# In the second token group x is loaded whole, x1 and h stay on chip, and the residual, norm and gelu work is placed anew

## The reference

```
mod = silu(cond) @ w_ada + b_ada -> sh1, sc1, g1, sh2, sc2, g2
h   = rms_norm(x, norm1_g) * (1 + sc1) + sh1
z   = h @ w_in            # q, k, v of two attentions, and gate logits
merged = sigmoid(ga) * (o_g @ w_branch_a) + sigmoid(gb) * (o_d @ w_branch_b)
x1  = x + g1 * (merged @ w_out)
h2  = rms_norm(x1, norm2_g) * (1 + sc2) + sh2
q   = h2 @ peer_w_query   # 8 heads, two halves of 128
per token and head: scores against 2 x 128 sub keys, the 16 best pairs -> expert ids, softmax weights
a   = gelu(h2 . peer_u[id]);  peer = sum (a * weight) * peer_v[id]
y   = rms_norm(x1 + g2 * peer, final_norm_g)
```

## Time and profile before

| | before |
|---|---|
| median of 3 runs | 5130.7 us (5129.67 to 5141.64) |
| the profiled execution | 5127.9 us, of which the span of the trace is 5126.2 us |
| PE, DVE, POOL, ACT busy | 65%, 53%, 36%, 9% |
| mean granted TensorE clock | 0.773 of full speed |
| bytes moved | 1885.14 MB, mean 368 GB/s |
| u and v gathers (software queue) | 1347.98 MB |
| weights and other transfers of SP | 535.33 MB |

### The profile page before, as it was taken

One profiled execution on the slowest core, in us unless ns is written; L12 is line 12 of the kernel. 1 busy time (PEld: TensorE's weight loads), 2 busy tenths in 40 slices (PEclk: granted clock), 3 DMA queues, 4 the chain that ended last, 5 costly groups with the idle time before them and its releaser, 6 DMA issues.

```text
span 5126.2 us, 33046 instructions
## 1 busy us (share of the span) xinstructions
PE 3345.8 (65%) x11402; PEld 1296.8 (25%) x11402; DVE 2718.6 (53%) x4111; ACT 455.3 (9%) x824; POOL 1835.9 (36%) x1365
## 2 busy tenths in 40 slices
PE   5969988999787798899988293333333333333334
PEld 0333343444344443444443141000000000000000
DVE  2320139986133202566758768565656556565653
ACT  0010010000222101111110011000000000000000
POOL 0000014432232000243534445545545564545542
PEclk7979999999899999999998696555555555555555
DMA  9979987997998688888989998999999999999997
GB/s 376 381 272 353 371 302 293 344 356 314 406 366 322 239 288 295 351 354 345 383 340 397 358 391 321 422 421 421 421 414 416 421 421 421 418 413 421 421 421 318
DMA packets 412276, 1885.14 MB, mean 368 GB/s; under 512 B 30544, under 2 KB 34160, under 8 KB 241760
## 3 DMA queue, kind: packets, MB, share of 16 engines
q0 software_dynamic: 187200, 1347.98, 64.6%
q1 hardware_dynamic: 224928, 535.33, 28.2%
HBM read 1845.08 MB, written 39.42 MB: 368 GB/s over the span
## 4 chain that ended last, share of the span: by engine, by line
DMA 52%; PE 27%; DVE 11%; issue 6%; POOL 3%; ACT 1%; SPq 0%; DVEq 0%; POOLq 0%; ACTq 0%; PEldq 0%
DMA activations<-in_peer_v,zt 33%; PE ps L821 20%; DMA big<-in_peer_u,sel 5%; DMA big<-in_peer_v,zone 4%; DMA big<-in_w_in 3%; DMA big<-in_peer_v,sel 2%; DVE big L1657 2%; DMA big<-in_w_ada 2%; PE ps L1167 2%; DMA big<-in_w_out 1%; DVE big L1604 1%; PE ps L921 1%; PE ps L981 1%; PE ps L872 1%; POOL big L753 1%
## 5 line engine op out<-in xcount | busy, mean ns | idle before, releaser
L821 PE MATMUL ps<-big,activations 128*128 128x512 f32 x4096 | 1809.3, 602 | 103.2 <-DMA big<-in_w_out 36.7
L1937 DVE CUSTOM_DVE_ANT_0 big<-big,activations 128x2048 f32<-128x2048 f32 x384 | 876.5, 2290 | 710.2 <-DMA big<-in_peer_u,sel 710.1
L821 PEld LDWEIGHTS ps<-big,activations 128*128 128x128 f32 x4096 | 781.7, 193 | 1114.7 <-issue 1017.3
L1167 PE MATMUL ps<-activations,zt 128*32 128x512 f32 x1536 | 354.3, 1014 | 569.9 <-DMA activations<-in_peer_v,zt 569.9
L805 POOL DMA_INDIRECT big<-in_peer_u,sel x384 | 501.1, 1305 | 603.4 <-DVE zt L1937 513.6
L1167 PE MATMUL ps<-big,zt 128*32 128x512 f32 x1536 | 328.8, 981 | 400.7 <-DMA big<-in_peer_v,zt 298.5
L1592 DVE CUSTOM_DVE_ANT_0 big<-big 128x2048 f32<-128x2048 f32 x128 | 291.5, 2292 | 128.0 <-DMA big<-in_peer_u,sel 113.4
L1604 DVE SCALAR_TENSOR_TENSOR big<-big,work 128x2048 f32<-128x2048 f32 x128 | 301.0, 2352 | 83.7 <-DMA big<-in_peer_v,sel 80.7
L809 POOL DMA_INDIRECT big<-in_peer_v,zt x192 | 279.0, 1453 | 177.9 <-PE ps L1167 128.8
L753 POOL DMA_INDIRECT big<-in_peer_u,sel x128 | 214.5, 1676 | 329.2 <-DVE work L1592 270.9
L753 POOL DMA_INDIRECT big<-in_peer_v,sel x128 | 237.9, 1859 | 254.6 <-DVE big L1604 186.7
(11 more groups left out here) (193 smaller groups left out, 2452.8 us busy)
## 6 DMA issues: line engine op xcount, KB each, us to landing
big<-in_w_in SPq DMA_DIRECT2D x84, 2048.0 KB, 10.3
big<-in_w_ada SPq DMA_DIRECT2D x48, 2048.0 KB, 12.8
big<-in_w_out SPq DMA_DIRECT2D x24, 2048.0 KB, 13.0
big<-in_peer_w_query SPq DMA_DIRECT2D x24, 2048.0 KB, 9.5
big<-in_w_branch_a SPq DMA_DIRECT2D x12, 2048.0 KB, 12.5
big<-in_w_branch_b SPq DMA_DIRECT2D x12, 2048.0 KB, 9.4
big<-z_blocks SPq DMA_DIRECT2D x20, 512.0 KB, 12.2
big<-in_peer_u,sel POOLq DMA_INDIRECT x640, 13.2
```

The lines of the kernel that those rows point to most:

```text
L821: ins = nc.tensor.matmul(bank(bk), acts[:, k, b * P:(b + 1) * P], w[:, n % WS, k], start=(start and k == 0), stop=(stop and k == KT // 2 - 1))
L1167: ins = nc.tensor.matmul(ps[32 * j:32 * j + 32, q * 512:(q + 1) * 512], spread[(t - 1) % 2][:, k * 32:(k + 1) * 32], v_slot(m)[:, j * CH:( ...
L1937: V.tensor_tensor_reduce(out=x, in0=x, in1=h_of[ph], scale=1.0, scalar=0.0, op0=ALU.mult, op1=ALU.add, accum_out=dots_s[t % 2][:, k:k + 1] ...
```

## The change

In group 2 only, and at the start and the end of the last stage:

- x of the three blocks is loaded whole (three transfers of 1 MB) as soon as the branch units are done, together with the rows of the second norm; the twelve pieces per chunk are gone. g1 comes after, and DVE waits for it at the first residual instead of before step 12.
- `residual_2` adds into the x buffer on chip, so that x1 stays there, and a third instruction takes the sum of squares of the chunk. x1 is still stored to `x1d`, for the last stage.
- `norm_2` adds up the four sums, takes the root, waits until the block's four stores of x1 have landed, and writes h over x1. The loads of x1, the stores of h and the loads of h are gone: `h_of` are the same buffers.
- The residuals stand at hand-picked places in steps 12 and 13 (`beside`), the norms at the 18th, 22nd and 24th place of step 13; step 14 has none. The gelus of ACT move with them.
- In the last stage the v buffers are free from the start (two of them are others than before); the final of block 0 moves from the end of step 0 to the fifth dot of step 1, and POOL waits for it before v gather number 6, because the gate row lies in that buffer. SP waits for it before it loads the rows and x1 pieces of the quarters.
- For the last block, PE does the sums of quarters 0 to 2 between the products of the last step.

```diff
@@ SP, group 2
+                    sp.wait_ge(mm_done, U_OUT[2])
+                    for lb in range(n):
+                        sp.dma_start(xb[lb], xs[block_of(g, lb)]).then_inc(G["xt"][lb], 16)
+                    sp.dma_start(A, mod[cnd:cnd + 1, 4 * D:5 * D].to_broadcast([P, D])).then_inc(s["row"], 16)
+                    sp.dma_start(Bv, mod[cnd:cnd + 1, 3 * D:4 * D].to_broadcast([P, D])).then_inc(s["row"], 16)
...
-                        sp.dma_start(zn(D + lb * CH, CH), xs[block_of(g, lb)][:, c * CH:(c + 1) * CH]).then_inc(G["xt"][lb], 16)
...
-                    for lb in range(2):
-                        sp.dma_start(xb[lb], x1d[block_of(g, lb)]).then_inc(s["x"][lb], 16)
-                    for lb in range(n):
-                        sp.wait_ge(s["h"], lb + 1)
-                        sp.dma_start(h2d[lb], h).then_inc(h2_out, 16)
...
-                        sp.wait_ge(t_done, 4 * (T_H[2] + GROUP[2]))
-                        sp.wait_ge(h2_out, 16 * GROUP[2])
-                        sp.dma_start(h_of[0], h2d[0]).then_inc(h_in[0], 16)
+                        sp.wait_ge(s["h"], n)
+                        sp.dma_start(fin_x, x1d[0]).then_inc(fa_in, 16)
@@ POOL, last stage
+                        if m == VR - V_LATE:
+                            pool.wait_ge(y_ready, 2)
@@ PE, last stage
+                    if t == STEPS_3 and k in (6, 10, 14):
+                        last_fold((k - 6) // 4)
@@ ACT, group 2
-                        if g == 2 and v in (2, 8):
-                            step = PH + 4 + v // 6
+                        elif v >= 4:
+                            sa.wait_ge(G["ou"], B * DCH + v - 3)
+                        if g == 2 and v in (0, 8):
+                            step = PH + 4 + v // 8
@@ DVE
+                def residual_2(v):
+                    c, lb = v // n, v % n
+                    x1 = nbuf[2][0][lb][:, c * CH:(c + 1) * CH]
+                    if v == 0:
+                        dve.wait_ge(G["g1"], 16 * (1 + B))
+                    dve.wait_ge(bank_free, U_OUT[2] + v + NB + 1)
+                    link(V.tensor_tensor(zt[:, v % 4], zt[:, v % 4], zn(c * CH, CH), ALU.mult))
+                    if c == 0:
+                        dve.wait_ge(G["xt"][lb], 16)
+                    link(V.tensor_tensor(x1, x1, zt[:, v % 4], ALU.add))
+                    signal(V.tensor_tensor_reduce(out=zt[:, v % 4], in0=x1, in1=x1, ..., accum_out=small[:, 40 + 4 * lb + c:41 + 4 * lb + c]), G["ou"], B * DCH + v + 1)
+                def norm_2(lb):
+                    link(V.tensor_reduce(small[:, 2:3], small[:, 40 + 4 * lb:44 + 4 * lb], AX.X, ALU.add))
+                    signal(V.tensor_scalar(small[:, 0:1], small[:, 2:3], 1.0 / D, EPS, ALU.mult, ALU.add), nrm_ms, nth)
+                    dve.wait_ge(nrm_rs, nth)
+                    link(V.reciprocal(small[:, 3:4], small[:, 1:2]))
+                    dve.wait_ge(G["br_st"][lb], 16 * 2 * DCH)
+                    link(V.scalar_tensor_tensor(x1[lb], x1[lb], small[:, 3:4], A, ALU.mult, ALU.mult))
+                    signal(V.tensor_tensor(x1[lb], x1[lb], Bv, ALU.add), nrm[2]["h"], lb + 1)
...
+                    beside = ({15: [(residual_2, 0)], 16: [(residual_2, 1)], 17: [(residual_2, 2)],
+                               25: [(residual_2, 3)], 27: [(residual_2, 4)], 30: [(residual_2, 5)]},
+                              {8: [(residual_2, 6)], 10: [(residual_2, 7)], 12: [(scale_row,)], 13: [(residual_2, 8)],
+                               18: [(residual_2, 9), (norm_2, 0)], 20: [(residual_2, 10)], 22: [(residual_2, 11), (norm_2, 1)],
+                               24: [(norm_2, 2)]})
...
+            dve.sem_inc(v_free, VR)
...
+                    if k == 4 and t == 1:
+                        dve.wait_ge(fa_in, 112)
+                        final(fin_x, fin_gate, fin_gain, 2)
...
-                if t == 0:
-                    dve.wait_ge(fa_in, 112)
-                    final(ac(A1, D), ac(A1 + D, D), ac(A1 + 2 * D, D), 2)
-                    dve.sem_inc(v_free, VR)
```

More of the change, by code:

```diff
@@ L91 @@
 UR, VR = 8, 8
+V_LATE = 2
 U_EARLY = WS * HALF // D
@@ L1406, in _ @@
                         scored(v - 2)
-                    if g == 2 and v == 8:
-                        top_exps(2 * PH)
-                        gelus(1, (PH + 7) * 2 * TOPK)
+                    if g == 2 and v in (2, 9):
+                        step = PH + 6 + v // 9
+                        top_exps(step + 1)
+                        gelus(1, step * 2 * TOPK)
                 if g < 2:
```

92 lines of the change are left out of this document (43 added, 49 removed).

## The result

| | before | after |
|---|---|---|
| median | 5130.85 us (5129.67 to 5141.64, 4 runs) | 5088.77 us (5080.02 to 5095.19, 4 runs) |
| profiled execution, its span | 5127.9, 5126.2 us | 5090.43, 5088.5 us |
| bytes | 1885.14 MB | 1875.70 MB |

The ratio is 0.9913, 95% interval 0.9899 to 0.9928: faster by 42 us, where 56 was forecast. Run again later (the tenth experiment), the kernel after gave 0.9919.

A forecast was written before the change was run, and what follows sets the result against it. The last stage is byte-bound; before it, DVE's stops fill the ring of four gathers and halt POOL. Steps 37, hand-over 9 and end 10 sum to 56 us: 5075 us, own range 5062 to 5086, eight in ten 5052 to 5102.

The forecast's parts named there:

- Step 12: Block 0's expert step 12: without the g1 wait, dots begin near 2609 and the step ends at 2737, against 2748.
- two queues taking turns: Step 12's dots: gathers and SP's large rows alternate, 10 transfers each in 50 us, the last dot ending at 2669.
- Step 13: Block 0's step 13 takes over the norms, with a 5.9 us store wait: 138 us, ending at 2875 against 2862.
- Steps 14 and 15: Block 0's last two steps: ends at 2988 and 3089, say 3090, 37 us earlier than 3127.
- the 2.9 with 7.5 for its loads: Step 14: 32 gathers at 2.9 us, choice 12.7, and 7.5 us for three 1 MB loads for the final.
- I take 2.75 us for a gather: Step 15, with weights nearly through: 88 us of gathers plus 12.7 of choice, 101 us.
- The rival of the unchanged rate: Gathers and weights together stay at 364 GB/s, step 15 ends at 3107, total 5092 us; chance 0.2.
- PE: Beside DVE's steps: query projection starts near 2862, scores end at 3047, 43 us ahead of step 15.
- the slower rival: More gathers starve PE's weights; at 36 us for each half the program takes 5178 us; chance 0.03.
- The hand-over: Start of the last stage: early v gathers and the moved final give 9 us beyond the steps' 37.
- The drain in front of v6: Hand-over: the DMA drains for some 17 us while POOL waits for the final; today about as long before v0.
- The end: Kernel's end: three of four last-block quarters pass between the last 16 products, saving 10 us, 4 as the low end.

The follow-up runs named there:

- the tenth experiment: The kernel after, unchanged, run again beside the kernel with later norms and the final in step 0: 5091.0 us, ratio 0.9919 to the kernel before.
- experiment 5: The kernel before with one edit, DVE waiting for g1 at its first residual instead of ahead of step 12: 5140.83 us, ratio 1.0011.
- experiment 8: The kernel after, with POOL issuing each gather of step 15 one buffer later, three in flight instead of four: 5108.35 us, ratio 0.9943.
- experiment 7: The kernel after, with SP also storing the three h blocks (3.1 MB) that nobody reads: 5091.72 us, ratio 0.9915 to the kernel before.
- experiment 2: The kernel after, with the final of block 0 behind step 0 again and the v buffers freed only there: 5097.93 us, ratio 0.9937.
- experiment 4: The kernel after, with the final of block 0 before the fifth dot of step 0 instead of step 1: 5085.41 us, ratio 0.9912.
- experiment 1: The kernel after, with all four sums of the last block behind PE's last product again: 5096.3 us, ratio 0.9926 to the kernel before.

## Why the prediction was right, and where it was off

The median of 5088.8 us lies in the wide range, 5052 to 5102, and outside the forecast's own, 5062 to 5086; it is 14 us above the forecast.

**Step 12** began at 2607.4, forecast 2609, and ended at 2740.9, forecast 2737. The forecast of two queues taking turns was right to the row: 4.97 us from dot to dot, and the last dot ended at 2670, forecast 2669. The reason for the gain was only half right. I put the gain down to the wait for g1, and experiment 5 shows that this wait covered a longer one, for PE's first unit; without the new places the edit is worth nothing. My sum used both edits, so its number stood; for the reason that I gave, that was luck.

**Step 13** ended at 2876.4, forecast 2875, and its store wait was 6.8 us, forecast 5.9. The Trainium skill's two terms for a transfer ("DMA: Bandwidth & Descriptors", anatomy of one DMA) give an estimated 2.6 us here, which would have made the wait 5 us too short. The page fitted them to transfers issued from GpSimd, which these stores, issued by SP, are not. The trace doesn't agree with them beside other transfers: the twelve stores took 9.2 us in the median.

**Steps 14 and 15** are where the forecast failed: 118.3 and 108.7 us against 113 and 102, 12 of the 13 us by which the steps fell short of 3090 (step 12 was longer, its start earlier and step 13 shorter than forecast, 1 us net). The steps that failed are "I take 2.75 us for a gather" in step 15, and in step 14 the 2.9 with 7.5 for its loads. They failed for two reasons.

In step 15 a gather took 2.9 to 3.0 us. I took the pace from the DMA's side: fewer bytes beside it, so faster gathers. The DMA is not full there (share 0.88, 339 GB/s), and experiment 8 takes one buffer away and the step grows by 18 us: the round of four buffers limits the pace. At the 421 GB/s of the last stage the step's 36.9 MB would take 88 us, by estimate, and with the 12.7 of the choice 100, about my number; the ring took the rest.

In step 14 the DMA is full, and by the one profile of experiment 7 the bytes do set the length. My 113 us for them ask for more than any rate seen here: the 48.0 MB of the step in 113 us are 425 GB/s. The error lies in the 2.9, from which I had taken off six residuals, 8.7 us, as if they had been on the path. They stood in a step whose DMA was full already (share 1.01 in the earlier trace rows), so taking them away could save little. Without that subtraction the step would be 114 + 7.5 = 121.5 us, by estimate; it was 118.3.

The rival of the unchanged rate (364 GB/s, 5092) came nearest, 3 us off, and its condition is what happened: by the windows the bytes from 2607 to 3103 went at 367 GB/s, not at the 377 of the forecast.

**PE** kept to the forecast as far as the query projection: h at 2827.75, 2847.70 and 2858.07 (forecast 2825, 2845, 2857), the projection at 2862.4 (2862). The scores ended at 3064, not 3047. The gelu at unit 9 did not have "15 us to spare": DVE was late, ACT waited, and PE stood 14.21 us behind ACT. Nothing followed, since the scores were 39 us ahead. No chunk waited for weights over 8.48 us, so the slower rival had nothing to start from. The prediction's estimate that weights beside gathers get a fifth of 421 GB/s, 25 us for a half, was too low: in step 14 SP's queue, most of it weights, moved 14.4 of the 48 MB, three tenths of 406 GB/s.

**The hand-over** gave 7.6 of 9, and experiment 2 measures 8.9 for the move of the final. The drain in front of v6 that I counted as lost is real but shorter than I had it: the DMA moves nothing for 6.6 us, not 17, and 5.0 us are gained without it in experiment 4. **The end** gave 7.0 of 10. The 10.4 behind the last product were as forecast; not in my sum was that from the last gather's issue to the last product it now takes 3.4 us more, 2.3 of it due to the folds between the products (experiment 1). For the other 1.1 no run gives a cause.

In sum 23.1 + 7.6 + 7.0 = 37.7, against 37 + 9 + 10 = 56. The mechanism was right for step 13's wait, for PE, the hand-over and the end. It was wrong for the g1 wait, where it cost nothing, and for what paces steps 14 and 15, which is 12 of the 18 us that are missing.

## What to carry to other kernels

Before you cost the removal of a wait, ask what the waiting engine does next: here 25 us of waiting for a row hid 33 us of waiting for PE, and the gain came only when the work was put where its input was due. Before you turn saved bytes, or saved work, into time in one stage, look at the DMA's share in that stage: with a full one (step 14) the length is the bytes over the rate, and work taken off DVE gives little; with gaps and a small ring (step 15) the number of buffers sets the pace, and saved bytes give little. And place an instruction that needs a store to have landed a store's time behind it: one place later took 7 us off a step.

## What the runs showed of the hardware

The landing of one gather grows with what is under way: 7.4 us with three gathers in flight, 8.3 with four, 10.5 with four and weights beside them. So the fourth buffer gave a fifth more pace (3.5 to 2.9 us), not a third. Step 14, with a full DMA, moved 405 to 406 GB/s in each profile of these steps, the last stage 421.

How long POOL takes to issue a gather goes with what DVE is doing. At the hand-over of the kernel after:

```profile
3150.59 2.29 DVE L1974 CUSTOM_DVE_ANT_0 big<-big,activations 128x2048 f32<-128x2048 f32 x1
3152.80 0.29 DVE L1542 MAX8 work<-work 128x8 f32<-128x128 f32 x1
```

```profile
3151.78 1.91 POOL L796 DMA_INDIRECT big<-in_peer_u,sel  x1 [0.30 <-issue]
3155.24 0.94 POOL L796 DMA_INDIRECT big<-in_peer_u,sel  x1 [0.30 <-issue]
```

The first is issued beside a dot, the second beside the small instructions of the choice. Over the whole trace of this kernel, 482 gathers were issued while DVE was in an instruction over 2048 elements a partition, and 407 of them took over 1.2 us, 2.2 in the median; of the 536 issued beside none, 9 did, and the median is 0.94. Whether POOL had waited makes less of a difference: where it had stood for over 1 us, 125 of 566 took over 1.2 us, else 293 of 714. That the two engines hinder each other is what this suggests; no run here changes one of them alone.
